# A decoder step on one core: logits first, corrections side by side, and the sample tokens' rows in four row groups

## The reference, cut to what matters

```python
h = layer_norm(DN_ALPHA * h + mix, g1, b1)
return layer_norm(DN_ALPHA * h + hier_moe(h, ...), g2, b2)

def hier_moe(h, w_r1, b_r1, w_r2, b_r2, w_gate, w_up, w_down):
    g_prob = jax.nn.softmax((xt @ w_r1).astype(F32) + b_r1, axis=-1)     # 4 groups
    p_grp, grp = lax.top_k(g_prob, 1)
    e_all = jnp.einsum('nd,gde->nge', xt, w_r2).astype(F32) + b_r2       # 4 experts in each
    e_logit = jnp.take_along_axis(e_all, grp[:, :, None], axis=1)[:, 0]
    p_e, e_idx = lax.top_k(jax.nn.softmax(e_logit, axis=-1), TOP_IN_GROUP)
    p_e = p_e / jnp.sum(p_e, -1, keepdims=True)
    gate = ...at[..., expert].add(p_grp * p_e)
    hid = jax.nn.silu(x @ w_gate[e]) * (x @ w_up[e])                     # for every expert
    y = jnp.einsum('nef,efd->nd', hid * gate, w_down)
```

## Time and profile before

| | us |
|---|---|
| median of three runs | 2512.09 (2508.17 to 2515.15) |
| the profiled execution | 2504.79 |
| its span | 2503.2 |
| TensorE busy | 2341.8 (94%) |
| VectorE busy | 663.3 (26%) |
| ScalarE busy | 501.5 (20%) |
| mean granted TensorE clock | 0.967 of full speed |

### The profile page before, as it was taken

How to read it: one execution, slowest core, us unless ns; L and a number is a source line. 1 busy time by engine, 2 the same in 40 slices (tenths; PEclk the granted TensorE clock), 3 DMA queues, 4 the chain that set the end, 5 groups by cost and what they waited for, 6 DMA issues and landing times.

```text
span 2503.2 us, 32244 instructions
## 1 busy us (share of the span) xinstructions
PE 2341.8 (94%) x12521; PEld 1443.3 (58%) x12521; DVE 663.3 (26%) x1245; ACT 501.5 (20%) x1125; POOL 4.2 (0%) x10
## 2 busy tenths in 40 slices
PE   6999999989999999898989998999999999999997
PEld 4768786678643434343568876645786343434345
DVE  0159911601551121212210000022025412121213
ACT  1120106510320101010210014633004200101014
POOL 0000000000000000000000000000000000000000
PEclk9999999989899999999989999999899999999999
DMA  8624457783149898989635446998440699989890
GB/s 272 188 78 158 145 168 232 224 304 135 68 178 428 341 429 346 429 360 429 247 107 163 147 153 212 358 338 288 173 164 34 281 391 380 424 359 429 363 392 35
DMA packets 210136, 647.70 MB, mean 259 GB/s; under 512 B 56841, under 2 KB 90266, under 8 KB 184154
## 3 DMA queue, kind: packets, MB, share of 16 engines
q1 hardware_dynamic: 174650, 636.31, 65.8%
q10 hardware_dynamic: 35376, 9.91, 1.7%
HBM read 640.19 MB, written 5.96 MB: 258 GB/s over the span
## 4 chain that ended last, share of the span: by engine, by line
PE 74%; DMA 13%; SPq 4%; ACT 3%; DVE 2%; ACTq 2%; issue 2%; DVEq 0%
PE bank L606 17%; PE bank L1180 11%; PE bank L1029 9%; PE bank L1165 8%; PE bank L1210 7%; DMA ring<-in_w_down 6%; DMA ring<-in_w_up 5%; PE bank L1224 5%; PE bank L784 3%; SPq L389 3%; ACTq L389 1%; PE bank L793 1%; ACT arena L1295 1%; PE bank L924 1%; PE bank L1085 1%
## 5 line engine op out<-in xcount | busy, mean ns | idle before, releaser
L1180 PE MATMUL bank<-ring,AT 128*64 128x512 f32 x2048 | 451.2, 599 | 27.6 <-DMA ring<-in_w_up 25.8
L1295 ACT ACTIVATE arena<-bank 128x512 f32<-128x512 f32 (+3 forms) x523 | 258.0, 542 | 946.8 <-PE bank L606 414.7
L606 PE MATMUL bank<-X,ring 128*128 128x264 f32 x1664 | 373.8, 388 | 1.2 <-ACT arena L1295 1.2
L606 PEld LDWEIGHTS bank<-X,ring 128*128 128x128 f32 x1664 | 317.8, 191 | 56.1 <-ACT arena L1295 1.4
L1180 PEld LDWEIGHTS bank<-ring,AT 128*64 128x64 f32 x2048 | 147.0, 138 | 323.0 <-issue 287.6
L1210 PE MATMUL bank<-ring,arena 128*64 128x512 f32 x1024 | 233.3, 612 | 32.7 <-DMA ring<-in_w_down 23.7
L1029 PE MATMUL bank<-AT,ring 128*128 128x264 f32 x1024 | 239.1, 397 | 7.1 <-DVEq L1861 7.1
L1029 PEld LDWEIGHTS bank<-AT,ring 128*128 128x128 f32 x1024 | 200.6, 196 | 43.7 <-issue 7.9
L2092 DVE TENSOR_TENSOR X<-bank,X 128x264 f32<-128x264 f32 x256 | 110.7, 433 | 395.3 <-PE bank L1224 392.4
L1165 PE MATMUL bank<-arena 128*128 128x256 bf16 (+1 forms) x1440 | 191.1, 273 | 0.5 <-DVE arena L1947 0.5
L1210 PEld LDWEIGHTS bank<-ring,arena 128*64 128x64 f32 x1024 | 77.0, 140 | 178.7 <-issue 155.6
(11 more groups left out here) (304 smaller groups left out, 1458.9 us busy)
## 6 DMA issues: line engine op xcount, KB each, us to landing
ring<-in_w_gate SPq DMA_DIRECT2D x64, 2048.0 KB, 17.1
ring<-in_w_up SPq DMA_DIRECT2D x64, 2048.0 KB, 13.0
ring<-in_w_down SPq DMA_DIRECT2D x64, 2048.0 KB, 16.7
ring<-in_w_o SPq DMA_DIRECT2D x16, 2048.0 KB, 10.4
ring<-in_cache_b_k SPq DMA_DIRECT2D x128, 256.0 KB, 4.2
ring<-in_cache_b_v SPq DMA_DIRECT2D x128, 256.0 KB, 4.9
ring<-in_w_in_a SPq DMA_DIRECT2D x14, 2048.0 KB, 9.1
ring<-in_w_in_b SPq DMA_DIRECT2D x12, 2048.0 KB, 8.3
```

The costliest lines, as they stand in the source:

```text
L606: mm = pe.matmul(B[4 * (g % 2) + f][:, 0:n_tok], u[:, c * 512 + f * P:c * 512 + (f + 1) * P], src[8 * half + c][:, 0:n_tok], start=(half = ...
L1180: mm = pe.matmul(B[bank][64 * s:64 * s + 64, :], M.xsT[:, at:at + 64], ring[slots[s][0]][:, c * FE:(c + 1) * FE], start=(half == 0 and c = ...
L1295: return act.activation(out, in_, ACT.Copy, scale=scale)
```

## The change

Four things change in the expert stage.

- **Logits first.** TensorE transposes the logits after the rows of item 0 and not after those of items 0 to 3. On VectorE the choice no longer waits for the exponentials: the second expert is found on the shifted logits, and the gate values are computed in a new function `gates`, after the low parts.
- **Corrections side by side.** The items are numbered by blocks of tokens (n = 4t + q), so that four corrections in a row stand on four row groups of the array; each of the first seven items has a bank of its own. The idle products ahead of the ranks are gone; there are six ahead of the gather (they were four).
- **The sample tokens' rows in four row groups.** They are computed as one item (n = 8), from values that VectorE has corrected beforehand (two small steps in `mix`, three after the choice), with 64 small products that put the rows at partitions 0, 32, 64 and 96, a quarter of the features at each. N_ITEMS falls from 10 to 9.
- **The gather.** It works in two halves of four banks each (GATHER_BANKS, six banks in turn). A half begins with the 24 products of the sample rows, one row group and one bank after the other, and then does the 48 of the full blocks bank by bank. The second half waits for two copies.

```diff
-N_ITEMS = 10
-ROW_BANKS = [4, 5, 6, 0]
+N_ITEMS = 9
+ROW_BANKS = [4, 5, 6, 0, 1, 2, 3, 4, 5]
+GATHER_BANKS = [2, 3, 4, 5, 6, 7, 2, 3]
...
-            if n < 8:
-                q, t = divmod(n, 2)
-                g, h = divmod(q, 2)
-                cols = slice(1024 * g, 1024 * (g + 1))
-            else:
-                q, t, h, cols = 3, 2, n - 8, slice(0, 1024)
-            blocks = [M.part[t][k][:, cols].rearrange("r (j p) -> r j p", j=8) for k in range(3)]
+            if n == 8:
+                return 0, 2, [M.part[2][k].rearrange("r (g j p) -> r g j p", g=2, j=2) for k in range(3)]
+            t, q = divmod(n, 4)
...
-                bank = B[ROW_BANKS[n % 4]]
-                pe.wait_ge(S("ln_scaled"), KC * layer + (4 * q + 4 if t < 2 else KC))
-                if n >= 4:
-                    pe.wait_ge(S("rest_made"), N_ITEMS * layer + n - 3)
+                bank = B[ROW_BANKS[n]]
+                pe.wait_ge(S("ln_scaled"), KC * layer + 4 * q + 4)
+                if n >= 7:
+                    pe.wait_ge(S("rest_made"), N_ITEMS * layer + n - 6)
...
+            def sample_rows(layer):
+                bank = B[ROW_BANKS[8]]
+                pe.wait_ge(S("terms_ready"), 2 * layer + 2)
+                pe.wait_ge(S("rest_made"), N_ITEMS * layer + 2)
+                for c in range(KC):
+                    for g in range(4):
+                        columns = ident.rearrange("k (p j) -> k p j", j=8)[:, :, 2 * g:2 * g + 2]
+                        mm = pe.matmul(bank[32 * g:32 * g + NB, 32 * c:32 * c + 32], M.xs[:, c * NB:(c + 1) * NB], columns,
+                                       start=True, stop=True)
+                mm.then_inc(S("token_rows"), 1)
...
-                for n in range(4):
-                    raw_rows(layer, n)
+                raw_rows(layer, 0)
                 pe.wait_ge(S("logits_copied"), layer + 1)
...
-                pe.wait_ge(S("fix_ready"), layer + 1)
+                for n in range(1, 4):
+                    raw_rows(layer, n)
+                pe.wait_ge(S("terms_ready"), 2 * layer + 1)
                 pe.wait_ge(S("gain_rows"), 32 * (layer + 1))
                 for n in range(4):
                     fix_rows(layer, n)
                 for n in range(4, 6):
                     raw_rows(layer, n)
-                    fix_rows(layer, n)
-                idle_products(4)
                 pe.wait_ge(S("chosen"), layer + 1)
...
-                for n in range(6, N_ITEMS):
+                for n in range(6, 8):
                     raw_rows(layer, n)
+                for n in range(4, 8):
                     fix_rows(layer, n)
-                idle_products(4)
+                sample_rows(layer)
+                pe.wait_ge(S("rest_made"), N_ITEMS * layer + 4)
+                idle_products(6)
                 pe.wait_ge(S("low_made"), N_ITEMS * (layer + 1))
...
-                    for q in range(8):
-                        if q >= 4:
-                            pe.wait_ge(sm("gather_copied"), done * 8 + (q - 3))
-                        for c in range(2):
-                            for t in range(3):
-                                at = (2 * q + c) * P
-                                rows = slice(0, P)
-                                if t == 2:
-                                    rows, at = slice(64 * (q // 4), 64 * (q // 4) + NB), at % 1024
-                                for k in range(3):
-                                    mm = pe.matmul(B[2 + q % 4][:, c * 2 * P:(c + 1) * 2 * P],
-                                                   M.part[t][k][rows, at:at + P], M.sel[rows, t * 2 * P:(t + 1) * 2 * P],
-                                                   start=(t == 0 and k == 0), stop=(t == 2 and k == 2))
-                        mm.then_inc(sm("gathered"), 1)
+                    for half in range(2):
+                        if half:
+                            pe.wait_ge(sm("gather_copied"), done * 8 + 2)
+                        banks = GATHER_BANKS[4 * half:4 * half + 4]
+                        for k in range(3):
+                            for c in range(2):
+                                at = (2 * half + c) * P
+                                for g in range(4):
+                                    rows = slice(32 * g, 32 * g + NB)
+                                    pe.matmul(B[banks[g]][:, c * 2 * P:(c + 1) * 2 * P], M.part[2][k][rows, at:at + P],
+                                              M.sel[rows, 4 * P:6 * P], start=(k == 0 and c == 0), stop=False)
+                        for g in range(4):
+                            for c in range(2):
+                                at = (8 * half + 2 * g + c) * P
+                                for t in range(2):
+                                    for k in range(3):
+                                        mm = pe.matmul(B[banks[g]][:, c * 2 * P:(c + 1) * 2 * P],
+                                                       M.part[t][k][:, at:at + P], M.sel[:, t * 2 * P:(t + 1) * 2 * P],
+                                                       start=False, stop=(c == 1 and t == 1 and k == 2))
+                            mm.then_inc(sm("gathered"), 1)
...
                     gather(it + 1)
+                    pe.wait_ge(sm("gather_copied"), it * 8 + 13)
                     turn_hidden(it, 1)
...
                 act.wait_ge(S("row_scale"), layer + 1)
-                router_exp(0)
                 row_high(layer, 0)
                 row_high(layer, 1)
-                router_exp(1)
+                router_exp(0)
                 for n in range(2, N_ITEMS + 2):
                     if n < N_ITEMS:
                         row_high(layer, n)
                     row_mid(layer, n - 2)
+                    if n == 3:
+                        router_exp(1)
...
+                samples = M.xs.rearrange("p (c b) -> p c b", b=NB)
+                shifts = M.xs_shift.rearrange("p (c b) -> p c b", b=NB)
+                gain = lnp[:, 16 * layer:16 * layer + KC].unsqueeze(2).broadcast_to((P, KC, NB))
+                by_token = lambda x: x.unsqueeze(1).broadcast_to((P, KC, NB))
+                link(dve.tensor_tensor(shifts, gain, by_token(M.sh[:, SEQ:T]), ALU.mult))
                 dve.wait_ge(S("ln_square_used"), 16 * k_ln + KC)
                 dve.scalar_tensor_tensor(M.rstd, M.sqs, -1.0, B[1][:, 0:T], ALU.mult, ALU.add).then_inc(S("ln_var"), 1)
                 dve.wait_ge(S("raw_logits"), layer + 1)
                 dve.scalar_tensor_tensor(M.lgT, M.sh[0:20, :], M.lb[:, 0:1], B[2][0:20, 0:T], ALU.mult, ALU.add)\
                    .then_inc(S("logits_copied"), 1)
+                dve.wait_ge(S("ln_scaled"), KC * (layer + 1))
+                link(dve.tensor_tensor(samples, Xv[:, :, SEQ:T], shifts, ALU.subtract))
...
+                link(dve.scalar_tensor_tensor(ep, o1, NEG, ep, ALU.mult, ALU.add))
+                dve.tensor_reduce(v2, ep, AX.X, ALU.max).then_inc(S("r_shifted"), 1)
...
-                link(dve.tensor_scalar(den, v2, 1.0, None, ALU.add))
-                link(dve.reciprocal(den, den))
-                link(dve.tensor_tensor(w1, den, pg, ALU.mult))
-                link(dve.tensor_tensor(w2, v2, w1, ALU.mult))
-                link(dve.tensor_tensor(tmp, o1, b3(w1, 4), ALU.mult))
-                link(dve.tensor_tensor(t4, o2, b3(w2, 4), ALU.mult))
-                link(dve.tensor_tensor(tmp, tmp, t4, ALU.add))
...
-                for n in range(3):
-                    lows(layer, [n])
-                    rests(layer, [n + 2])
+                lows(layer, [0])
+                link(dve.reciprocal(M.xs_scale, M.rstd[:, SEQ:T]))
+                samples = M.xs.rearrange("p (c b) -> p c b", b=NB)
+                bias = lnp[:, 32 + 16 * layer:32 + 16 * layer + KC].unsqueeze(2).broadcast_to((P, KC, NB))
+                link(dve.tensor_tensor(samples, samples, M.xs_scale.unsqueeze(1).broadcast_to((P, KC, NB)), ALU.mult))
+                dve.tensor_tensor(samples, samples, bias, ALU.add).then_inc(S("terms_ready"), 1)
+                rests(layer, [2])
+                lows(layer, [1])
+                rests(layer, [3])
...
+            def gates(layer):
+                dve.wait_ge(S("r_exp"), 2 * layer + 2)
+                link(dve.tensor_reduce(sum_, ge, AX.X, ALU.add))
+                link(dve.reciprocal(pg, sum_))
+                link(dve.tensor_scalar(den, e2, 1.0, None, ALU.add))
+                link(dve.reciprocal(den, den))
+                link(dve.tensor_tensor(w1, den, pg, ALU.mult))
+                link(dve.tensor_tensor(w2, e2, w1, ALU.mult))
+                link(dve.tensor_tensor(tmp, o1, b3(w1, 4), ALU.mult))
+                link(dve.tensor_tensor(t4, o2, b3(w2, 4), ALU.mult))
+                link(dve.tensor_tensor(tmp, tmp, t4, ALU.add))
+                link(dve.tensor_tensor(gate, tmp.unsqueeze(2).broadcast_to((P, 3, 4, 4)),
+                                       og.unsqueeze(3).broadcast_to((P, 3, 4, 4)), ALU.mult))
...
```

(4 more changed lines are left out.)

109 lines of the change are left out of this document (55 added, 54 removed).

## The result

The changed kernel takes 2423.64 us, the median of four runs (2421.33 to 2428.49), against 2510.13 us for the kernel before on the same chip (2506.86 to 2515.15, four runs). The ratio is 0.9656, with an interval of 0.9633 to 0.9679. The forecast was 2428 us in a range of 2408 to 2462, so time and sign came out as predicted.

A forecast was written before the change was run, and what follows sets the result against it. TensorE was taken to set each quad's length, with weight transfers needing some 118 of 127.46 us. Savings of 56 (loop), 13 (first gathers) and 15 us (routing), 84 in all, from the 2512.1 us median gave 2428 us, range 2408 to 2462.

The forecast's parts named there:

- The gather: Each of ten gathers: 12.0 us after the change instead of 19.1, 7.0 less, with 8-row products four side by side.
- bounds of 1.3, 2.6 and 5.1 us: Time of a gather's 48 8-row products if four, two or none run side by side; four was taken.
- The rival of fewer groups side by side: In the gather, only two row groups (2441 us) or none (2466 us) run side by side; chance 0.12.
- The loop: Expert loops: eight passes (quads), each 7.0 us shorter, from 127.46 to 120.5 us, saving 56 us.
- The rival of the loads: Expert loop: weight loads take over, longer waits give back 28 us, ending at 2456 us; chance 0.12.
- What the forecast said of the down products: Expert loop: down products have no DMA wait, since their weights came during the gather.
- The first gathers: The gather ahead of each layer's expert loop: 7.0 us shorter, counted as 6.5 per layer, 13 us.
- a tie with the number of quads: Loop start: number of quads ready 12.8 us after the low parts, gather with last copy 12.9; 6.5 us counted per layer.
- Routing: Routing stage ahead of the first gathers: 9 us earlier in layer 0, 6 in layer 1; 15 taken, bounds 3 to 24.
- The middle between 2.4 and 1.2 GHz: Layer 0 routing: gather 13.4 us earlier at 2.4 GHz, 5 at 1.2 GHz; the middle, 9 us earlier, was taken.
- The rival that the clock eats the routing gain: Routing stage: the clock leaves a gain of 3 us instead of 15, ending at 2440 us; chance 0.10.
- The one on the slow side: Gather: each 8-row product takes 0.273 us instead of 0.107, 4.8 us more per gather, ending at 2545 us; chance 0.04.

The follow-up runs named there:

- the three traces above: Traces of the changed kernel (2423.64 us) and of it with each block's 8-row products on one row group (2483.62 us) or two in turn (2432.48 us).
- group after group: Changed kernel with each block's 24 8-row products ordered six on one row group, then six on the next, instead of one on each in turn: 2436.34 us.

## Why the prediction was right, and where its steps were not

**The gather, right in mechanism and size.** Predicted 12.0 us from 96 full products, 12 turns of four and four switches; measured 12.1. The choice between bounds of 1.3, 2.6 and 5.1 us for the 48 products of 8 rows fell on the first, and the three traces above show each of them. The rival of fewer groups side by side does not hold. Another order would have given nearly its price: group after group costs 1.4 us per gather. The Trainium skill, "TensorE: Matmul & The Clock Gate", in its table on small-K matmuls, has 3.07 for four groups of K=32 (at 512 columns; here 8 rows and 256 columns). The measurement decides for 4.0 once the switch is taken out, and 3.6 with it (2.72 against 0.76 us). The same page of the Trainium skill, under "The mechanism", says that tiles of different row groups overlap with starts some 4 ns apart and that products keep the program's order. The trace agrees with the first: four 8-row products start at 788.289, .292, .296 and .299 us, the next four 0.12 us behind, and each four after that 0.109 us behind. It doesn't agree with the second: group after group in the program's order would be 2.4 us a block, and it took 1.47. There the measurement decides.

**The loop, 56 us predicted, 53.7 measured.** Quads of 120.5 us were forecast, and 121.9 came. The 127.46 us that the forecast took for a quad of before is a window cut 2.07 us short; that quad is 129.5 us (the others of layer 0 130.5, 127.4 and 129.0, and 127.0 to 130.2 in layer 1). The difference is what was right, 6.7 us on average, of 6.9 by which the gather got shorter. The rival of the loads (28 us given back) is false at this length: the waits for weights went from 6.2 to 6.3 us a quad. It begins below it: of the next 5.2 us a quarter is lost. The term was mis-sized by 2.3 us. Of these 0.7 are the gather itself (6.9 for 7.0, eight times) and 0.5 the waits for weights; the rest goes with ScalarE's waits, 1.1 us a quad before and 1.3 after. What the forecast said of the down products, that they have no DMA wait, holds for those behind the gather only: those of the first pair wait 1.06 and 2.69 us in the second quad, and did so before the change (1.07 and 2.70).

**The first gathers, 13 us predicted, 7.1 measured.** This is the step that failed. The text set 7.0 less for the first gather, cut to 6.5 by a tie with the number of quads, and the tie was not what decided: the products wait for ScalarE's copy (0.87 us), and the number is ready at 697.1 us. The prediction worked out the end of the six idle products for 1.2 GHz alone (691 us), where they cover the last low parts. For 2.4 GHz it had the low parts' end and not that TensorE runs out of work ahead of it. In the trace the idle products end at 682.7 us, TensorE stands still for 2.51 us and runs the next 6.8 us at 1.2 GHz: 3.2 and 3.3 us lost in the two layers, 6.5 in all. Nine idle products bring the gather to 12.3 us and these 6.5 us back.

**Routing, 15 us predicted, 21 measured** (12.1 in layer 0, 8.7 in layer 1, from the first row product to the gather's start; taken 9 and 6). The ranks start 11.0 us earlier after the first row product (22.0 to 11.0 us), as predicted. What was priced too high lies behind them. The middle between 2.4 and 1.2 GHz was taken, and in the trace the clock fell for one stretch only: the rows of the last two items took 3.66 us, while ranks (2.48 us) and both sets of corrections (1.14 us) ran at 2.4 GHz. The 64 small products for the sample rows, priced at up to 6 us by L1122's, took 1.25 us for 128 instructions. The last low part ends at 685.19 us, inside the predicted 682.8 to 686.6.

So two terms were off with opposite signs, +6 and -6, and the sum of 84 us stood against 81.5 for 20.7, 7.1 and 53.7: right partly by luck. Layer by layer it is the same: 15.5 us were forecast for routing and first gather of layer 0 and 15.7 measured, 12.5 and 12.2 for layer 1, each from two parts of which neither was right.

**The rival that the clock eats the routing gain** had 0.10. In the profiled run of the change it took 6.5 of 21 us. Without the new gather it took all of it by the median of ten runs. It was better founded than its chance said. The one on the slow side (0.273 us for each 8-row product) has nothing in any trace: the price of a change of row group is 3 to 4 ns.

## What to carry to other kernels

Small products that use few rows are worth a place in different row groups, but it is the order that brings it: go round the groups with each product, because one group behind the other was no better here than two groups. Before you price a stretch by its products, look at whether TensorE stands still ahead of it: here 2.51 us of that cost 3.2 us on a gather of 12.3, and once 14.8 us on one of 19.1, and three more idle products took it away. A wait for a load inside a loop doesn't tell that the loads set its length: with 6.2 us of such waits in a quad, a gather shorter by 6.9 us still gave 6.7. Nearer to the transfers' own length, from 121.9 us down, a cut of 5.2 us gave 3.9.
